# Two-block transformer on one core: a shared item for two key projections, the last merged sum on the vector engine, meta keys' value products on the full height of the array

## What is computed

```python
proj = jnp.einsum('bsd,de->bse', hn, w_in[l])
(a_q, a_k, a_v, i_q, i_k, i_w, b_cq, b_ckv, b_kr, g_a, g_b) = jnp.split(proj, IN_OFFSETS, axis=-1)
...
i_k = apply_rope(rmsnorm(i_k, idx_k_norm_g[l])[:, :, None, :], cos_i, sin_i, IDX_ROT_DIM)[:, :, 0, :]
...
k_rope = apply_rope(b_kr[:, :, None, :], cos_b, sin_b, B_ROPE_DIM)[:, :, 0, :]
...
merged = jax.nn.sigmoid(g_a) * y_a + jax.nn.sigmoid(g_b) * y_b
h = h + jnp.einsum('bsd,de->bse', merged, w_out[l])
```

## Time and profile before

| | |
|---|---|
| time, three runs | 2308.83, 2309.58, 2315.37 us; median 2309.58 us |
| the profiled execution | 2314.37 us; span 2312.2 us |
| mean granted TensorE clock | 0.986 |
| PE busy | 2223.5 us (96%), 12432 matmuls |
| PEld busy | 1807.8 us (78%) |
| DVE busy | 1256.2 us (54%) |
| ACT busy | 902.9 us (39%) |
| POOL busy | 234.4 us (10%) |

### The profile page before, as it was taken

The page is one execution under the profiler, slowest core; times in us unless marked ns, Lnnn a source line. Parts: engine busy times, 40 slices in busy tenths (PEclk is TensorE's granted clock), DMA queues, the critical chain, the costliest instruction groups (busy, mean ns, idle before and its releaser), DMA issues.

```text
span 2312.2 us, 36243 instructions
## 1 busy us (share of the span) xinstructions
PE 2223.5 (96%) x12432; PEld 1807.8 (78%) x12432; DVE 1256.2 (54%) x2674; ACT 902.9 (39%) x1805; POOL 234.4 (10%) x199
## 2 busy tenths in 40 slices
PE   6999999989999999999999799999999999999998
PEld 4567766767888889999999677777776777888887
DVE  5878877457745755543443554544445555443442
ACT  3465444444423444322232344443444434322333
POOL 0100034420000012000001000112100041000001
PEclk7999999999999999999999899999999999999999
DMA  3111211234443342233333122234333233333332
GB/s 99 47 38 38 65 42 51 59 106 138 142 135 90 96 147 82 87 119 93 90 101 104 57 80 81 77 101 106 92 83 99 80 91 91 96 102 89 91 108 74
DMA packets 400423, 205.90 MB, mean 89 GB/s; under 512 B 68988, under 2 KB 393960, under 8 KB 400316
## 3 DMA queue, kind: packets, MB, share of 16 engines
q1 hardware_dynamic: 399397, 204.09, 30.9%
q10 hardware_dynamic: 919, 0.43, 0.1%
HBM read 202.21 MB, written 14.80 MB: 94 GB/s over the span
## 4 chain that ended last, share of the span: by engine, by line
PE 64%; issue 19%; DVE 4%; ACT 2%; POOL 1%; DMA 0%; SPq 0%; POOLq 0%; DVEq 0%; ACTq 0%
PE acc L1145 34%; PE acc L1431 15%; PE acc L1191 5%; PE sco L1466 2%; PE acc L1530 2%; PE acc L1526 1%; PE sco L1233 1%; DVE w_lo L2204 1%; PE sco L1506 1%; POOL vT L1078 1%; PE acc L1280 1%; PE acc L1506 0%; PE sco L1486 0%; POOL merged L1125 0%; PE acc L1267 0%
## 5 line engine op out<-in xcount | busy, mean ns | idle before, releaser
L1658 ACT ACTIVATE w_hi<-raw 128x512 fp32r<-128x512 f32 (+3 forms) x658 | 372.9, 614 | 694.2 <-PE acc L1145 657.5
L2204 DVE TENSOR_TENSOR w_lo<-raw,w_hi 128x512 fp32r<-128x512 f32 (+3 forms) x658 | 427.4, 689 | 143.4 <-ACT w_hi L1658 140.4
L1145 PE MATMUL acc<-xn_hi,w_hi 128*128 128x512 f32 (+1 forms) x1408 | 419.9, 339 | 2.1 <-DVE qbuf L2739 2.1
L1145 PE MATMUL acc<-xn_lo,w_hi 128*128 128x512 f32 (+1 forms) x1408 | 421.1, 340 | 0.0
L1145 PE MATMUL acc<-xn_hi,w_lo 128*128 128x512 f32 (+1 forms) x1408 | 420.6, 340 | 0.0
L1145 PE MATMUL acc<-hid_hi,w_hi 128*128 128x512 f32 (+1 forms) x832 | 260.7, 348 | 11.0 <-DVE hid_lo L2681 11.0
L1145 PEld LDWEIGHTS acc<-xn_hi,w_hi 128*128 128x128 f32 x1408 | 242.3, 188 | 35.7 <-DVE qbuf L2739 3.0
L1145 PEld LDWEIGHTS acc<-xn_hi,w_lo 128*128 128x128 f32 x1408 | 241.8, 188 | 29.9
L1145 PEld LDWEIGHTS acc<-xn_lo,w_hi 128*128 128x128 f32 x1408 | 240.6, 188 | 31.2 <-issue 0.5
L1145 PE MATMUL acc<-hid_lo,w_hi 128*128 128x512 f32 (+1 forms) x832 | 262.4, 350 | 0.0
L1145 PE MATMUL acc<-hid_hi,w_lo 128*128 128x512 f32 (+1 forms) x832 | 261.3, 348 | 0.0
(11 more groups left out here) (387 smaller groups left out, 3063.8 us busy)
## 6 DMA issues: line engine op xcount, KB each, us to landing
raw<-in_w_ffn_in SPq DMA_DIRECT2D x176, 256.0 KB, 3.0
raw<-in_w_in SPq DMA_DIRECT2D x118, 256.0 KB, 3.1
raw<-in_w_up SPq DMA_DIRECT2D x88, 256.0 KB, 3.0
raw<-in_w_ffn_out SPq DMA_DIRECT2D x32, 384.0 KB, 3.3
raw<-in_w_gate SPq DMA_DIRECT2D x48, 256.0 KB, 3.1
raw<-in_w_ffn_out SPq DMA_DIRECT2D x32, 320.0 KB, 3.7
raw<-in_w_out SPq DMA_DIRECT2D x32, 256.0 KB, 3.0
bias<-grids_dram SPq DMA_DIRECT2D x64, 128.0 KB, 2.9
```

Source lines behind the costliest of these rows:

```text
L1145: mm = pe.matmul(acc[0:m, 2 * slot + b, 0:size], w[slot][:, t, 0:m], x[:, place(t), c:c + size], start=(t == 0 and w is w_hi and x is xh), ...
L1658: act.activation(w_hi[slot][:, a:b, :], raw[slot][:, a:b, :], ACT.Copy).then_inc(S[f"hi_ready{slot}"], parts)
L2204: dve.tensor_tensor(w_lo[slot][:, a:b, :], raw[slot][:, a:b, :], w_hi[slot][:, a:b, :].bitcast(F32), ALU.subtract).then_inc(S[f"split{slot ...
```

## The change

1. `bkr` is no item any more. `ik` loads 72 columns and, as a second transfer, the 32 of `b_kr` to columns 96 to 127, and runs 128 columns wide; ACT takes it in three activations (before: two for `ik`, one for `bkr`). The front has 62 items, not 63, so every later item is on the other slot. The steps that stood in `bkr` now stand in `cq0`, those of `cq0` in `cq1`; the rotation of `ik`, before in the middle of `cq1`, follows it.
2. The last sum of each merged tensor (tile 7, branch A1 and branch C2) is made by DVE (`last_sum`) right after the scaling, in place of the one-element copy and POOL's sum; `hid_hi` of tile 7 waits for the new semaphore `last_added`.
3. The meta keys' value products in the mixers run over all 128 partitions: POOL writes zeros into the four buffers at the start of the mixers, and DVE waits for it (`meta_zero`).
4. SP issues the first turn of "proj_out" in straight code and loops over the other three.
5. Counts of semaphores and rotations are fitted to it.

The core of the diff (the fitted counts, and the helper `roped_item`, which gives `ik` for "bkr", are left out):

```diff
-    ik, bkr, cq0, cq1 = add("ik", "I", 0), add("bkr", "I", 0), add("cq", "I", 0), add("cq", "I", 1)
+    ik, cq0, cq1 = add("ik", "I", 0), add("cq", "I", 0), add("cq", "I", 1)
...
     order.extend([("now", ik), ("square", "ik"), ("xcopy", 0)])
-    whole(bkr, [("nsum", "ik"), ("vecs", 0), ("root", "ik")])
+    whole(cq0, [("nsum", "ik"), ("vecs", 0), ("root", "ik")])
     order.extend([("angles", 1), ("iw", 0)])
-    whole(cq0, [("sines", 0), ("lines", 0)])
-    whole(cq1, ("rope", ik))
-    order.append(("square", "cq"))
-    whole(iq0, [("nsum", "cq"), ("root", "cq"), ("rope", bkr)])
+    whole(cq1, [("sines", 0), ("lines", 0)])
+    order.extend([("rope", ik), ("square", "cq")])
+    whole(iq0, [("nsum", "cq"), ("root", "cq"), ("rope", "bkr")])
     order.append(("hi", "cq"))
...
-        meta_pairs = [pt[0:META, :, 0, :], raw[0][0:META, KT:KT + 2, :]]
+        meta_pairs = [pt[:, :, 0, :], raw[0][:, KT:KT + 2, :]]
...
-                column = {"ik": "i_k", "bkr": "b_kr", "cq": "b_cq", "ckv": "b_ckv", "iq": "i_q"}.get(kind)
+                column = {"cq": "b_cq", "ckv": "b_ckv", "iq": "i_q"}.get(kind)
                 if column:
-                    first = IN1[column] + P * at - (64 if kind == "bkr" else 0)
-                    rows(slot, k, win1, first, tiles, {"ik": 72, "bkr": 96}.get(kind, P))
+                    rows(slot, k, win1, IN1[column] + P * at, tiles)
+                elif kind == "ik":
+                    load(slot, k, [(raw[slot][:, 0:KT, 0:72], win1[:, :, bass.ds(IN1["i_k"], 72)]),
+                                   (raw[slot][:, 0:KT, 96:P], win1[:, :, bass.ds(IN1["b_kr"], 32)])])
...
-                    n.loop(0, 4, turn)
+                    n.straight(0, turn)
+                    n.loop(1, 4, turn)
...
+                            made = roped_item(j)
+                            pool.wait_ge(S[f"acc_free{made % 2}"], n.at(f"acc_free{made % 2}", k_of_item(made)))
                             pool.wait_ge(S["roped"], n.at("roped", ROPES[j]))
                             pool.tensor_tensor(rope_x[0:rows, :], x, cos[0:rows, :], ALU.mult).then_inc(S["cos_done"], 1)
-                        elif what == "dense" and FRONT_ITEMS[j][0:2] == ("branch", "A1"):
+                        elif what == "dense" and FRONT_ITEMS[j][0:2] == ("branch", "A1") and FRONT_ITEMS[j][2] < KT - 1:
                             m = FRONT_ITEMS[j][2]
                             pool.wait_ge(S["y_done"], n.at("y_done", m + 1))
                             pool.tensor_tensor(gates_b[m], gates_b[m], gates_a[m], ALU.add).then_inc(S["added"], 1)
...
+                    for ev in ("xn_ready", "split0"):
+                        pool.wait_ge(S[ev], n.at(ev, 0))
+                    for rest in (*meta_pairs, *(x[:, 0:1, :] for x in values_of)):
+                        last = pool.memset(rest, 0.0)
+                    last.then_inc(S["meta_zero"], 1)
...
-                        elif what == "dense" and ITEMS[j][0] == "branch" and part[1] == 4 and ITEMS[j][1] != "A2":
+                        elif (what == "dense" and ITEMS[j][0] == "branch" and part[1] == 4 and ITEMS[j][1] != "A2"
+                              and ITEMS[j][1:3] != ("C2", KT - 1)):
                             sums += 1
...
-                    for k, place, size in [*seen, (0, 0, META)]:
+                    seen = [(k, 1 + b) for b, k in enumerate(seen_tiles(t) if name == "C2" else range(1, 5))]
+                    for k, place in [*seen, (0, 0)]:
                         for hh in range(heads):
                             keys = meta_of(v + hh) if place == 0 else pt[:, (v + hh) % 2, place, :]
-                            source = values_of[keys_at(name, i)][0:size, k, :]
+                            source = values_of[keys_at(name, i)][:, k, :]
...
                     if kind == "ik":
+                        act.activation(key_raw[0:64, :], acc[0:64, slot, :], ACT.Copy)
                         act.activation(key_raw[64:72, :], acc[64:72, slot, :], ACT.Copy, scale=8 ** -0.5)
-                        act.activation(key_raw[0:64, :], acc[0:64, slot, :], ACT.Copy).then_inc(free, 1)
-                    elif kind == "bkr":
-                        act.activation(kr_raw, acc[0:96, slot, :], ACT.Copy).then_inc(free, 1)
+                        act.activation(kr_raw[64:96, :], acc[96:P, slot, :], ACT.Copy).then_inc(free, 1)
...
-                        act.wait_ge(S["added"], n.at("added", k + 1 - KT))
+                        last = k == KT - 1
+                        act.wait_ge(S["last_added" if last else "added"],
+                                    n.at("last_added", 0) if last else n.at("added", k + 2 - KT))
                         act.activation(hid_hi[:, merged_tile(ph[1], k), c0:T], merged[:, k, c0:T], ACT.Copy).then_inc(
                             S["xhi_ready"], 1)
...
+            def last_sum(term):
+
+                dve.tensor_tensor(merged[:, KT - 1, META:T], merged[:, KT - 1, META:T], term, ALU.add).then_inc(
+                    S["last_added"], 1)
...
+                        if name == "A1" and at == KT - 1:
+                            b = FRONT_ITEMS.index(("branch", "B1", at, 4))
+                            dve.wait_ge(S[f"acc_free{b % 2}"], n.at(f"acc_free{b % 2}", k_of_item(b)))
+                            dve.wait_ge(S[f"acc_free{slot}"], n.at(f"acc_free{slot}", k))
+                            last_sum(gate)
+                        elif name == "A1":
...
-                        dve.tensor_copy(small[0:1, 69:70], small[0:1, 34:35]).then_inc(S["y_done"], 1)
+                        if name == "C2" and at == KT - 1:
+                            dve.wait_ge(S["added"], n.at("added", KT))
+                            last_sum(dst)
+                        else:
+                            dve.tensor_copy(small[0:1, 69:70], small[0:1, 34:35]).then_inc(S["y_done"], 1)
...
 
```

More of the change, by code:

```diff
@@ L243, in work_of_front @@
         if k == 1:
-            order.append(("first", bkr))
+            order.append(("first", cq0))
     order.extend([("now", ik), ("square", "ik"), ("xcopy", 0)])
-    whole(bkr, [("nsum", "ik"), ("vecs", 0), ("root", "ik")])
+    whole(cq0, [("nsum", "ik"), ("vecs", 0), ("root", "ik")])
     order.extend([("angles", 1), ("iw", 0)])
-    whole(cq0, [("sines", 0), ("lines", 0)])
-    whole(cq1, ("rope", ik))
-    order.append(("square", "cq"))
-    whole(iq0, [("nsum", "cq"), ("root", "cq"), ("rope", bkr)])
+    whole(cq1, [("sines", 0), ("lines", 0)])
+    order.extend([("rope", ik), ("square", "cq")])
+    whole(iq0, [("nsum", "cq"), ("root", "cq"), ("rope", "bkr")])
     order.append(("hi", "cq"))
@@ L301, in front_item, with roped_item @@
     return next(n for n, x in enumerate(FRONT_ITEMS) if x[0] == kind and x[2] == index)
+def roped_item(n):
+    return front_item("ik", 0) if n == "bkr" else n
 def score_of_rope(kind):
-    return ROPES[front_item(kind, 0)] + 1
+    return ROPES["bkr" if kind == "bkr" else front_item(kind, 0)] + 1
 def front_outputs(v):
@@ L832, in rope_of @@
         def rope_of(n):
-            kind, _, at, _ = FRONT_ITEMS[n]
+            kind, _, at, _ = ("bkr", "I", 0, KT) if n == "bkr" else FRONT_ITEMS[n]
             if kind == "bq":
@@ L845, in turned_into @@
         def turned_into(n):
-            if FRONT_ITEMS[n][0] == "ik":
+            if n == front_item("ik", 0):
                 return [index_keys[0:64, :], index_keys[64:P, :]], slice(0, 64)
-            if FRONT_ITEMS[n][0] == "bkr":
+            if n == "bkr":
                 return [kbuf[64:96, hh, META:T] for hh in range(2)], slice(64, 96)
@@ L1181, in dense @@
                         kind, outputs[name] if kind == "branch" else (xn_hi, xn_lo))
-                    m = {"ik": 72, "bkr": 96, "bq": 96}.get(kind, P)
+                    m = 96 if kind == "bq" else P
                     for t in range(first, end):
@@ L1203, in rope @@
                     x, matrix, _, _, rows = rope_of(j)
-                    if FRONT_ITEMS[j][0] == "ik":
+                    if j == front_item("ik", 0):
                         pe.wait_ge(S["key_ready"], n.at("key_ready", 1))
-                    taken(j)
+                    taken(roped_item(j))
                     pe.wait_ge(S["roped"], n.at("roped", ROPES[j]))
@@ L1519, in values @@
                     o = outputs_until(v) % 2 * P
-                    seen = [(k, 1 + b, P) for b, k in enumerate(seen_tiles(t) if name == "C2" else range(1, 5))]
-                    for k, place, size in [*seen, (0, 0, META)]:
+                    seen = [(k, 1 + b) for b, k in enumerate(seen_tiles(t) if name == "C2" else range(1, 5))]
+                    for k, place in [*seen, (0, 0)]:
                         for hh in range(heads):
                             keys = meta_of(v + hh) if place == 0 else pt[:, (v + hh) % 2, place, :]
-                            source = values_of[keys_at(name, i)][0:size, k, :]
+                            source = values_of[keys_at(name, i)][:, k, :]
```

13 lines of the change are left out of this document (6 added, 7 removed).

## The result

The changed kernel takes 2300.22 us (median of 6 runs, 2298.83 to 2301.11), the kernel before in the same comparison 2312.05 us (median of 6, 2308.83 to 2315.37). The ratio is 0.9948, 95% interval 0.9935 to 0.9961: faster by 12 us. A second comparison on another occasion gave 0.9946 (0.9933 to 0.9958). The profiled execution took 2298.83 us.

A forecast was written before the change was run, and what follows sets the result against it. PE, busy 2223.5 of 2312.2 us with mostly dense matmul, was taken as the bound, with DVE close behind from 60 to 80 us. Terms −2.9 − 3.6 − 0.5 − 9 + 2.5 = −13.5 from 2309.58 gave 2296 us, range 2289 to 2302.

The forecast's parts named there:

- 4.8 us were taken off: Base of the forecast: the profiled execution, 2314.37, lay 4.8 us above the runs' median, 2309.58, which was used instead.
- Part 3, −9 us: Mixers: full-height value products save 4.8 us in A2 and 4.5 in B2 and C2, taken as −9 (bounds −4, −11).
- the part lost to waits for other engines: Mixers: a twentieth of PE's 9.3 us saving may be lost to other engines, leaving 9.
- short matmuls would run beside each other for little: Mixers: if short matmuls overlapped for only the drain, the 4.5 us of B2 and C2 would be lost.
- Front's end, −3.6 us: Before the first proj_out: slot 1's load starts sooner, so PE's gap is 3.6 us instead of 7.2.
- Front's start, −2.9 us: Merged item: PE loses 5.6 us of matmuls, but DVE's chain lets only 2.9 arrive at `iq0`'s rotation.
- Clock, +2.5 us: Granted clock falls at one of two places behind new or longer gaps, making 13 matmuls cost 2.5 us more.
- Two places were named and one counted: Clock might fall at 68 us and behind the second proj_out's longer gap; one fall was counted, +2.5 us.
- Second proj_out, −0.5 us: No wait for tile 7 gives −1.1, the sum on DVE ahead of `w_lo` +0.6: −0.5 us in all.
- the one in which the clock falls at both places: Rival: clock falls at both the 68 us place and the second proj_out, time 2298.6 us; chance 0.2.
- the drains are paid back: Contrary rival, mixers: drains not paid back, short matmuls cheaper or savings waited away, 4 instead of 9, 2301 us; chance 0.15.
- PE's 5.6 us did not arrive at the start: Contrary rival, front's start: DVE is not the bound, so PE's 5.6 us arrive, time 2293.5 us; chance 0.1.

The follow-up runs named there:

- half: Changed kernel with the meta keys' value products over 64 partitions instead of 128: 2307.26 us, ratio 0.9975 to the kernel before.
- Item_only: Kernel before with part 1 alone and the slots that follow from it (zeros still written): 2309.36 us, ratio 0.9985 to the kernel before.
- zeros_only: Kernel before with part 3 alone (zeros, value products over 128 partitions): 2303.15 us, ratio 0.9965 to the kernel before.
- pool_sum: Changed kernel with part 2 undone (both last sums on POOL, one-element copy back): 2299.46 us, ratio 0.9938 to the kernel before.
- sum_inside: Changed kernel with DVE's last sum moved between the sixth and seventh `hid_lo`: 2297.43 us, ratio 0.9942 to the kernel before.
- both_again: Second run of the changed kernel with both rotations moved later and DVE's last sum between sixth and seventh `hid_lo`: 2294.29 us, ratio 0.9926.
- after_again: The changed kernel itself, unaltered, run once more: 2299.52 us, ratio 0.9946 to the kernel before.

## Why the prediction was right, and where its terms were off

The time lies in the range, and the direction is as forecast: −13.5 us predicted, −12 measured. Part of that closeness is luck, as the point on the clock shows. The forecast time, 2296, is 4 us low for two reasons. First, 4.8 us were taken off because the profiled execution lay that far above the median of three runs; with more runs the median of the kernel before is 2312 to 2313, so the execution was about 2 us above, and 2.5 of the 4 us are there. The rest is in the terms. Against the profiled executions, which the offsets compare, the change is −15.2 us and not −12.

- **Part 3, −9 us.** Measured 8 to 9. The steps were nearly exact: A2 0.37 us (taken 0.3), B2 and C2 0.145 (0.14). But with the exact ones PE saves 10.5, not 9.3, and the part lost to waits for other engines was taken as a twentieth where it was about a fifth: two errors that nearly cancel. The zeros cost nothing, as costed. The rule of the Trainium skill ("TensorEngine Tiling (Array Packing)", Key Properties) that a change of mode drains the engine agrees with "half": 1.39 us with 64 partitions as with 16, against 1.03 at full height. That short matmuls would run beside each other for little, the other side of that passage of the prediction, showed in no run.
- **Front's end, −3.6 us.** The gap fell from 7.18 to 3.54, by 3.64. "Item_only" shows that part 1 with its slots does it. The place gained 1.0 us more (the offset is −4.97 by 532 us), since some 8 steps, not 12, were at the lower clock. Of this offset 1.77 us are gone again by 1279 us, in dense matmuls without a wait; "zeros_only", whose code there is that of the kernel before, has the changed kernel's length in this stretch, so it is not the change. The cause is open.
- **Front's start, −2.9 us** before the clock. The new wait was forecast at some 3 us, behind the rotation of `ik`, and was 3.33; DVE had the key part 1.2 us earlier than forecast. But this was where the clock fell (so PE, not DVE, was the late one), and PE's rotation for `iq0` came 1.61 us earlier, not 2.9 (forecast for 77.6, found at 78.86). Most of this was gone by 342 us, for which the next point has the cause.
- **Clock, +2.5 us.** This step failed as a method. It had the length of one gap to go by: 2.92 us left the clock up in the kernel before. Behind 2.92 us in "pool_sum" and "item_only" (the first proj_out) the matmuls were long, and behind the 2.80 of "sum_inside" too; behind another 2.80 us at the same place, in "both_again", they were not:

```profile
465.90 0.47 PE L1162 MATMUL acc<-hid_hi,w_hi 128*128 128x512 f32 x1 [2.80 <-DVE hid_lo L2710]
```

Two places were named and one counted; in the changed kernel's trace the clock fell at both. Besides, it fell or stayed up in places that the change does not touch. Windows of the kernel before, then of the changed one:

```profile
326.00:336.00 10.00, 7.89 (x40) 4.76 (x39) 8.78 (x29) 3.35 (x8) 2.62 (x3) 0.83 0.01 2
1788.00:1798.00 10.00, 8.40 (x35) 5.74 (x36) 3.12 (x11) 1.88 (x5) 0.95 (x1) 0.66 0.30 81
```

```profile
326.00:336.00 10.00, 7.70 (x31) 4.82 (x32) 9.34 (x32) 3.64 (x9) 3.10 (x2) 0.66 0.00 1
1774.00:1784.00 10.00, 8.71 (x52) 6.49 (x51) 4.82 (x16) 3.88 (x12) 1.27 (x1) 1.00 0.39 108
```

From 326 to 336 us the clock is 0.83 before and 0.66 after, behind a wait for DVE of 2.11 and 2.46 us: this took 1.66 us back (the offset goes from −2.05 to −0.39), 0.35 of it the longer wait. In the kernel before it fell near 1790, behind a gap of 1.62 us, and in the changed one, behind 1.29 us at the same instruction, it did not: 2.8 us gained (the offset between the traces goes from −12.98 to −15.96 by 1797.6, 0.14 of it part 3's) that no part of the change makes. A third such place lies near 1322 us. The kernel before, then the changed one:

```profile
1322.36 0.27 PE L1486 MATMUL sco<-const,aux 128*16 128x128 f32 x1 [1.95 <-issue]
...
1324.17 0.64 PE L1431 MATMUL acc<-xn_lo,w_hi 128*128 128x264 f32 x2
```

```profile
1318.62 0.27 PE L1500 MATMUL sco<-const,aux 128*16 128x128 f32 x1 [1.95 <-issue]
...
1320.15 0.40 PE L1445 MATMUL acc<-xn_lo,w_hi 128*128 128x264 f32 x2
```

The gap is 1.95 us in both ("issue": the profile shows nothing that PE waited for), and only in the kernel before are the matmuls long behind it; the changed kernel gains 1.5 us here (the offset goes from −3.74 to −5.24). A second execution of the changed kernel ("after_again") shows that such places differ for one program:

```profile
326.00:336.00 10.00, 7.54 (x39) 4.81 (x39) 9.33 (x31) 4.18 (x10) 3.11 (x2) 0.83 0.00 1
```

The lower clock comes and goes between executions, so one trace pair is a sample. Over all runs the means give the changed kernel a clock lower by 0.0011, an estimated 2.3 us: in the mean the size of the term was about right, though the method could not say where.

- **Second proj_out, −0.5 us.** The gap of 3.50 was forecast at 3.5, and PE waits for no tile behind it. The place lost 1.9 us in all (the offset goes from −17.06 to −15.2); −0.5, and +2.5 where the clock falls, made +2.0. In the time part 2 alone cannot be told from nothing ("pool_sum").

Of the rivals, the one in which the clock falls at both places is what the trace shows, and its 2298.6 us is nearer to the measured 2300.22 than the forecast's 2296. In the trace 4.3 us gained by clock that happened to stay up, near 1322 and near 1790 us, stand against it; that is luck. The others are out: the drains are paid back, and PE's 5.6 us did not arrive at the start, where PE now waits for DVE.

## What to carry to other kernels

In a stretch where the second engine has 2 to 3 us of slack, matmuls that are taken off PE turn into a wait of that length (3.33 us here). Giving PE the next independent block first only moved the wait here (0.51 us at the old place, 2.46 at the next), so look for the next thing that waits for the same engine. Which slot the last item is in decides how early the next phase's weights can be loaded; count it before anything else when an item is added or taken away. A few low matmuls among full ones cost a change of height, so zeros that make them full can be cheaper. Before a difference of a few us is explained, compare the mean granted clock of the runs: 0.001 of it was worth about 2 us of 2300.

## What the runs showed of the hardware

- Matmuls over 64 partitions between matmuls over 128 cost what those over 16 do: A2 products 1.40 us with either, 1.03 with 128.
- The granted clock fell behind gaps of PE of 1.62 and 1.95 us (kernel before, near 1790 and 1322), 2.80 and 2.92 us ("sum_inside", "pool_sum"). It stayed up behind one of 1.95 us (changed kernel, the same instruction), one of 2.80 ("both_again", the same place as in "sum_inside") and one of 2.92 (second proj_out of the kernel before). The length of the gap alone does not say which. What does was not found.
- With DVE's `w_lo` pair 0.15 us ahead of POOL's sum the pair took 1.27 us and the sum, with DVE's `hid_lo` beside it, 6.49; where the pair was 0.07 us ahead it took 2.37 and the sum 1.74 (both in "pool_sum"). In these two places a tenth of a microsecond went with the exchange; that it decides is not shown.
